# Moving 8 of 24 modulation tiles from the attention loop to the projection loop, and reordering three groups of loads

## What is computed

```python
def adaln(c, w, b):
    m = jax.nn.silu(c) @ w + b
    m = m.reshape(c.shape[0], 1, 6, D_MODEL)
    return [m[:, :, k] for k in range(6)]
...
    xp = xp + mp[2] * op
```

```python
def mla_sample(h, past_lat, past_rope, w_in, q_g, kv_g, w_qb, w_kvb, w_o):
...
    k_lat = jnp.concatenate([past_lat, ckv], axis=1)
    k_pe = jnp.concatenate([past_rope, kr], axis=1)
    q = jnp.concatenate([q_lat, q_pe], axis=-1)
    k = jnp.concatenate([k_lat, k_pe], axis=-1)[:, :, None, :]
    o_lat = causal_attention(q, k, k_lat[:, :, None, :], t0)
```

## Time and profile before

| | us |
|---|---|
| median of 3 runs | 1580.44 (1579.52 to 1583.05) |
| the profiled execution | 1581.58 |
| its span | 1580.0 |
| PE busy | 1494.8 |
| DVE, ACT, POOL busy | 370.3, 260.1, 111.2 |
| DMA | 463.22 MB, mean 293 GB/s |

### The profile page before, as it was taken

The page is one execution under the profiler, slowest core; times in us unless marked ns, Lnnn a source line. Parts: engine busy times, 40 slices in busy tenths (PEclk is TensorE's granted clock), DMA queues, the critical chain, the costliest instruction groups (busy, mean ns, idle before and its releaser), DMA issues.

```text
span 1580.0 us, 24287 instructions
## 1 busy us (share of the span) xinstructions
PE 1494.8 (95%) x9928; PEld 885.9 (56%) x9928; DVE 370.3 (23%) x903; ACT 260.1 (16%) x586; POOL 111.2 (7%) x167
## 2 busy tenths in 40 slices
PE   6999877999999999999998999999999999998998
PEld 3544545788888878778785554553344234432342
DVE  2223431300000055634576100001000100011104
ACT  2122320200000022357503100000000000000001
POOL 1101550000000000000010100000000100010000
PEclk9999997999999999999999999999999999999999
DMA  9759987244334553472358899999999999999995
GB/s 379 306 214 392 365 289 240 107 162 160 122 105 146 197 189 120 155 263 94 147 211 349 288 348 379 392 408 401 421 417 419 405 420 417 420 404 419 418 418 220
DMA packets 104011, 463.22 MB, mean 293 GB/s; under 512 B 16110, under 2 KB 35339, under 8 KB 62261
## 3 DMA queue, kind: packets, MB, share of 16 engines
q1 hardware_dynamic: 91136, 420.49, 68.7%
q0 software_dynamic: 10256, 39.98, 7.3%
q10 hardware_dynamic: 2512, 1.23, 0.3%
HBM read 446.30 MB, written 15.55 MB: 292 GB/s over the span
## 4 chain that ended last, share of the span: by engine, by line
PE 76%; DMA 11%; DVE 5%; issue 4%; POOL 2%; ACT 1%; SPq 0%; POOLq 0%; DVEq 0%
PE bank L1622 11%; PE bank L1177 10%; PE bank L1147 8%; PE bank L1672 5%; PE bank L1191 5%; PE bank L1515 5%; DMA ring<-in_moe_w_up 4%; DMA ringx<-in_moe_w_up 3%; PE bank L1634 3%; PE bank L1225 3%; PE bank L1530 2%; PE bank L1556 2%; PE bank L890 2%; PE bank L924 2%; PE bank L977 2%
## 5 line engine op out<-in xcount | busy, mean ns | idle before, releaser
L1622 PE MATMUL bank<-ring,hg 128*32 128x512 f32 (+1 forms) x1456 | 208.5, 566 | 7.8 <-DMA ring<-in_moe_w_up 7.1
L1177 PE MATMUL bank<-hT,ring 128*128 128x264 f32 x704 | 156.9, 386 | 0.3 <-ACT hT L1725 0.3
L1622 PE MATMUL bank<-ringx,hg 128*32 128x512 f32 (+1 forms) x848 | 146.1, 568 | 3.8 <-DMA ring<-in_moe_w_up 2.8
L1177 PEld LDWEIGHTS bank<-hT,ring 128*128 128x128 f32 x704 | 133.7, 190 | 23.4 <-issue 0.6
L1622 PEld LDWEIGHTS bank<-ring,hg 128*32 128x32 f32 x1456 | 62.7, 111 | 110.3 <-issue 99.8
L1147 PE MATMUL bank<-hT,ring 128*128 128x264 f32 x512 | 118.7, 394 | 1.7 <-ACT hT L1725 1.3
L1147 PEld LDWEIGHTS bank<-hT,ring 128*128 128x128 f32 x512 | 99.1, 194 | 19.9 <-issue 2.1
L1672 PE MATMUL bank<-ring,turnH 128*32 128x512 f32 x768 | 92.6, 603 | 0.0
L1191 PE MATMUL bank<-actT,ring 128*128 128x264 f32 x352 | 79.1, 386 | 0.6 <-DVE actT L2210 0.6
L1515 PE MATMUL bank<-ring,hg 128*128 128x512 f32 (+1 forms) x192 | 78.0, 560 | 0.6 <-ACT hg L1940 0.6
L1622 PEld LDWEIGHTS bank<-ringx,hg 128*32 128x32 f32 x848 | 44.2, 112 | 59.6 <-issue 55.8
(11 more groups left out here) (565 smaller groups left out, 1787.4 us busy)
## 6 DMA issues: line engine op xcount, KB each, us to landing
ring<-in_moe_w_down SPq DMA_DIRECT2D x53, 1024.0 KB, 17.1
ring<-in_w_ada SPq DMA_DIRECT2D x48, 1024.0 KB, 11.2
ring<-in_moe_w_up SPq DMA_DIRECT2D x40, 1024.0 KB, 16.1
ring<-in_moe_w_gate SPq DMA_DIRECT2D x32, 1024.0 KB, 17.0
ringx<-in_moe_w_gate SPq DMA_DIRECT2D x27, 1024.0 KB, 12.8
ringx<-in_moe_w_down SPq DMA_DIRECT2D x24, 1024.0 KB, 18.1
ring<-in_ssm_w_in SPq DMA_DIRECT2D x20, 1024.0 KB, 4.9
ringx<-in_moe_w_up SPq DMA_DIRECT2D x19, 1024.0 KB, 15.9
```

The source lines that it names most:

```text
L1177: m = mm(bank[2 * w + q][:, 0:T], slot8(tl)[:, k, q * P:(q + 1) * P], hT[:, k, :], start=k == 0, stop=k == DC - 1)
L1622: m = mm(bank[2 * b_ + u][rows, 0:HALVES[g][u]], hg[:, k, rows], w[:, kk, 512 * u:512 * u + HALVES[g][u]], start=k == 0, stop=k == DC - 1, ...
```

## The change

The diff does four things. It gives the projection loop 32 tiles (2 or 3 at a time) and four turns, with heads 3, 7, 11 and 15, and the attention loop 8 tiles (heads 0 to 7) and one turn (head 9). On POOL the rotary keys of group two are loaded ahead of the token pages of sequences 1 to 3. The token pages of sequence 7 go from SP's queue to POOL's, behind `samp_scored` 3. On SP the four tiles WO go behind the token pages of sequences 4 to 6, and so behind `samp_scored` 3 too.

```diff
--- before.py
+++ after.py
@@ -60,7 +60,7 @@
 
 MOE = 134
 LAT_SLOTS = [n % NS for n in range(LAT, WO)]
-ADA_HEADS = [(0, 2), (2, 4), (4, 6), (6, 7), (7, 8), (8, 8), (8, 10), (10, 12), (12, 14), (14, 15), (15, 16), (16, 16), (16, 18), (18, 20), (20, 22), (22, 24)]
+ADA_HEADS = [(0, 3), (3, 6), (6, 8), (8, 8), (8, 11), (11, 14), (14, 16), (16, 16), (16, 19), (19, 22), (22, 24), (24, 24), (24, 27), (27, 30), (30, 32), (32, 32)]
 MS = 12
 GROUPS = [(512 * g, min(512, FF - 512 * g)) for g in range(-(-FF // 512))]
 NG = len(GROUPS)
@@ -490,20 +490,20 @@
         flat = rvar[:, 0:256] if n >= 6 else spare[n // 2][:, 2048:2304]
         return flat[:, n % 2 * PAGE:(n % 2 + 1) * PAGE]
 
-    def page_ids(eng, b0):
-
-        return [[eng.value_load(pages[0:1, b * NPG + n:b * NPG + n + 1], min_val=0, max_val=a["cache_kv_latent"].shape[1] - 1)
-                 for n in range(NPG)] for b in range(b0, b0 + 4)]
+    def page_ids(eng, which):
+
+        return {b: [eng.value_load(pages[0:1, b * NPG + n:b * NPG + n + 1], min_val=0, max_val=a["cache_kv_latent"].shape[1] - 1)
+                    for n in range(NPG)] for b in which}
 
     def load_turned(eng, ids_, b, n):
 
         out = turned_page(b, n)
-        src = a["cache_kv_turned"][ds(ids_[b % 4][n], 1), :, :].rearrange("a p (u t) -> (a p) u t", u=4 if b == 3 else KC)
+        src = a["cache_kv_turned"][ds(ids_[b][n], 1), :, :].rearrange("a p (u t) -> (a p) u t", u=4 if b == 3 else KC)
         return eng.dma_start(out, src)
 
     def load_tokens(eng, ids_, b, n):
 
-        src = a["cache_kv_latent"][0, ds(ids_[b % 4][n], 1), :, :]
+        src = a["cache_kv_latent"][0, ds(ids_[b][n], 1), :, :]
         src = src.rearrange("a p (u r) -> (a p) u r", u=4) if b == 7 else src.rearrange("a p r -> (a p) r")
         return eng.dma_start(token_page(b, n), src)
 
@@ -560,19 +560,19 @@
             fill8(IN0 + j, w, win0[:, j, 0:DC * w])
         ada(0, ADAR, 1, 3)
         sp.wait_ge(s["pool_in"], 16)
-        sample_pages = page_ids(sp, 4)
+        sample_pages = page_ids(sp, range(4, NB))
         ada(1, ADA1, 0, 3)
         for b in range(4, NB):
             for n in range(NPG):
                 if n == 0:
                     sp.wait_ge(s["units"], unit(LAT + b - 4 - NS))
                 load_turned(sp, sample_pages, b, n).then_inc(ring_ready[(LAT + b - 4) % NS], 16)
+        sp.wait_ge(s["samp_scored"], 3)
+        for b in range(4, NB - 1):
+            for n in range(NPG):
+                load_tokens(sp, sample_pages, b, n).then_inc(lat_ready[b], 16)
         for j in range(4):
             fill8(WO + j, 256, wo_d[:, j, :])
-        sp.wait_ge(s["samp_scored"], 3)
-        for b in range(4, NB):
-            for n in range(NPG):
-                load_tokens(sp, sample_pages, b, n).then_inc(lat_ready[b], 16)
         with sp.Fori(0, 2) as i:
             for j in range(4):
                 for w, src in enumerate((wg0, wu0)):
@@ -705,7 +705,7 @@
         g.memset(qpeT[:, :, H:32], 0.0).then_inc(s["zeroed"], 1)
         g.memset(qlatT[:, :, :, H:32], 0.0).then_inc(s["zeroed"], 1)
 
-        sample_pages = page_ids(g, 0)
+        sample_pages = page_ids(g, (0, 1, 2, 3, 7))
 
         def turned(b):
             for n in range(NPG):
@@ -730,14 +730,16 @@
         rope_keys(0)
         g.wait_ge(s["s_done"], DC)
         tokens(0)
+        g.wait_ge(s["ada_turned"], 6)
+        g.wait_ge(s["rope_in"], 64 + 16 * NPG)
+        rope_keys(1)
         g.wait_ge(s["s_done"], H)
         tokens(1)
         tokens(2)
         g.wait_ge(s["o_done"], H)
         tokens(3)
-        g.wait_ge(s["ada_turned"], 6)
-        g.wait_ge(s["rope_in"], 64 + 16 * NPG)
-        rope_keys(1)
+        g.wait_ge(s["samp_scored"], 3)
+        tokens(7)
         g.wait_ge(s["ltok_copied"], 3)
         g.dma_start(o[2][0, 0].rearrange("(c p) r -> p c r", p=P), ltok[:, 0:2, 0:KVR]).then_inc(s["out_done"], 16)
         g.dma_start(o[3][0, 0].rearrange("(c p) r -> p c r", p=P), ltok[:, 0:2, KVR:]).then_inc(s["out_done"], 16)
@@ -995,8 +997,8 @@
                 if tile and tile % DC == 0:
                     pe.wait_ge(s["ada_added"], 1 + tile // DC)
                 ada_tile(ADAR + tile, tile % DC, bank[3])
-            if h in (5, 11):
-                ada_turn((5, 11).index(h) + 1, bank[3][:, 0:144])
+            if h % 4 == 3:
+                ada_turn(h // 4 + 1, bank[3][:, 0:144])
         head_back(H - 1)
 
 
@@ -1036,30 +1038,24 @@
                            start=t == 0, stop=t == 1, skip_group_check=True)
             m.then_inc(s["o_done"], 2)
 
-        pe.wait_ge(s["ada_added"], 3)
+        pe.wait_ge(s["ada_added"], 5)
         scores(0)
-
-        def ada1_turn(blk):
-            ada_turn(3 + blk, bank[2][:, 144 * blk:144 * (blk + 1)])
 
         for h in range(H):
             if h + 1 < H:
                 scores(h + 1)
-            t = DC + h
-            if t == 2 * DC:
-                pe.wait_ge(s["ada_copied"], 6)
-            ada_tile(ADA1 + t, t % DC, bank[(3, 7, 3)[t // DC]])
-            if t % DC == 1:
-                ada1_turn(t // DC - 1)
+            if h < DC:
+                ada_tile(ADA1 + 2 * DC + h, h, bank[3])
+            if h == DC + 1:
+                ada_turn(5, bank[2][:, 0:144])
             turn_p(h)
             if h % 2 == 0 and h:
                 values(h // 2 - 1)
-        ada1_turn(2)
         values(H // 2 - 1)
 
 
         pe.wait_ge(s["o_copied"], H // 2)
-        pe.wait_ge(s["ada_added"], 4)
+        pe.wait_ge(s["ada_added"], 6)
 
         def sample_scores(g_):
 
@@ -2106,13 +2102,12 @@
         v.wait_ge(s["rope_in"], 64)
         v.tensor_scalar(rope_rows[:], pages_all[:], float(ROPE), cst[:, C_ROW:C_ROW + 1], ALU.mult, ALU.add)
         for h in range(H):
-            if h in (4, 10, 15):
-                blk = (4, 10, 15).index(h) + 1
+            blk = h // 4 + 1
+            if h % 4 == 2:
                 ada_rows(blk, ADAR + DC * blk - 1, bank[3])
-            if h in (5, 11):
-                blk = (5, 11).index(h) + 1
+            if h % 4 == 3:
                 v.wait_ge(s["ada_turned"], blk + 1)
-                ada_add(0, bank[3][:, 0:144], 16 * blk, 16 * blk + 16, blk + 1)
+                ada_add(blk // 3, bank[3][:, 0:144], 16 * (blk % 3), 16 * (blk % 3) + 16, blk + 1)
             v.wait_ge(s["q_rotated"], h + 1)
             v.wait_ge(s["q_copied"], h + 1)
             v.tensor_tensor(ropet[64:96, :], bank[4][64:96, 0:T], sin, ALU.mult)
@@ -2145,9 +2140,8 @@
             if h + 1 < H:
                 maxima(h + 1)
             normalise(h)
-            t = DC + h
-            if t % DC == DC - 1:
-                ada_rows(3 + t // DC, ADA1 + t, bank[(3, 7, 3)[t // DC]])
+            if h == DC - 1:
+                ada_rows(5, ADA1 + 3 * DC - 1, bank[3])
             if h >= 3 and h % 2:
                 pair = h // 2 - 1
                 v.wait_ge(s["o_done"], 2 * pair + 2)
@@ -2155,7 +2149,7 @@
         v.wait_ge(s["o_done"], H)
         v.tensor_copy(oT[:, H // 2 - 1, 0:TP], bank[(H // 2 - 1) % 2][:, 0:TP]).then_inc(s["o_copied"], 1)
         v.wait_ge(s["ada_turned"], 6)
-        ada_add(1, bank[2][:, 0:432], 0, 48, 4)
+        ada_add(1, bank[2][:, 0:144], 32, 48, 6)
 
 
         def sample_sums(g_):
```

## The result

The change makes the kernel slower: 1590.95 us in the median of 10 runs (1587.49 to 1595.73), against 1583.59 (1578.03 to 1589.18) for the kernel before, run beside it. The ratio is 1.0048, with a 95% interval of 1.0032 to 1.0065. The forecast was 1573.5, in a range of 1569 to 1581. The profiled execution took 1590.72 us with a span of 1588.8, 8.8 more than the span before.

What follows compares the result with a forecast made beforehand. It took PE's path to bound the kernel (76% of the chain), with a 12.2 us wait for rotary keys. +9.2 − 2.1 − 14.0 = −6.9 us, from the median 1580.44, gave 1573.5 us, range 1569 to 1581.

Steps and rivals of the forecast that it cites:

- the part on the attention loop: Attention loop: heads 8 to 14 gain nothing from losing a tile; last head and last turn save, sum −2.1 us.
- The first rival: Second half of attention loop: clock falls, 1.5 us a head, +12 for 8, so 1585.5 us; chance 10%.
- Projection loop, +9.2: Projection loop: 10 more tiles and one more turn cost +10.3 us, less 1.1 at its end.
- Last head and last turn, −2.1: End of attention loop: tile delaying transposes 1.0, turn holding values 0.85, shorter addition 0.3 us, all saved.
- Rotary wait, −12.2: Before second scoring of the sequences: PE's 12.2 us wait for rotary keys of group two goes whole.
- the clock of the second scoring, −1.8: `sample_scores(1)`: clock stays up without the wait, so 9.0 us instead of 10.8.
- Moved loads, 0, bound +5.1: Group two's token pages, WO, sequence 7: moving them costs nothing; pages at most 5.1 us late.
- the second rival: Values of group two: token pages come late, PE stands still, +1.5 to +5.1, 1575 to 1578.6 us; chance 18%.
- Supply of tiles, 0, bound +3: Projection loop: tiles behind SP's page numbers arrive in time with 2 us to spare; cost 0, at most +3.
- the sum −6.9: Whole kernel: +9.2 projection loop, −2.1 attention loop, −14.0 rotary keys and second scoring's clock.

Runs made afterwards that it cites:

- the second group: Four follow-up kernels run on one chip beside the kernel before: four idle products 0.9992, sequence 7 on SP 0.9982, output weights ahead 0.997, five idle products 0.9977.
- the third group: Four kernels run again unchanged on one chip beside the kernel before: seven idle products 0.9964, four 0.9969, own memory for rotary keys 0.991, that with five products 0.9926.

## Why the prediction was wrong

**The step that failed** is in the part on the attention loop: heads 8 to 14 "lose a tile each and gain nothing: the gap is only idle for 1.6 us". The gap was idle for 1.6 us, and PE's order of work stood as forecast. But the clock was taken to stay at 1.00. The first rival came instead. Its size was well priced in the sum: 12, against 10.7 + 2.1 = 12.8 measured for the loop. A pair took 11.05 − 7.4 = 3.65 us more, so 1.8 a head and not 1.5; but the clock fell late in the first of the eight heads, and the last has no scores of its own. The rival had left out 2.1 more for the first scoring: the low clock outlasted the gaps by some 5 us, with PE busy all the time (240 to 244). What was wrong was its chance of 10%. It rested on one row, 66 to 68 us in the earlier trace rows, with PE busy for 0.66 of 2 us at full clock: one gap by itself. Eight heads without a tile are another case. No row of the kernel before could have settled it. One of its stretches has PE almost as little busy as the change at 196 to 200 (2.72 of 4 us), and keeps its clock:

```profile
204.00:208.00 4.00, 2.85 (x24) 1.66 (x21) 2.34 (x10) 2.16 (x9) 0.00 (x0) 1.00 0.60 164
```

And with the tiles alone PE was busy 9.92 of 16 us at 1.00 before the clock fell. That the missing tiles are the cause is shown by the kernels with products in their place: 26.28 of 32 us busy at 1.00, with the same work of DVE and the same loads.

The Trainium skill, TensorE: Matmul & The Clock Gate, section A second HAM failure mode: psum-queue depth-cycling, says that frequent short idle times between groups of matmuls can make the clock go up and down. The trace agrees with the cause and not quite with the picture: 44 us at 0.50 in one piece (about 201 to 245), with no rise in between.

**Projection loop, +9.2:** right, with a little luck. The first scores came at 165.59, which is 7.8 later, and 1.35 of the start is to be added: +9.2. A third tile of a head took 0.86 us (2.71 for three, 1.85 for two), not 0.925, and a wait of 0.55 for a tile, counted as nothing, made up for most of that.

**Last head and last turn, −2.1:** right as far as it can be read. With products in the gaps the loop takes 62.0 us against 63.7 − 2.1 = 61.6.

**Rotary wait, −12.2, and the clock of the second scoring, −1.8:** right, both to a tenth.

**Moved loads, 0, bound +5.1:** low by 1.3 (1.9 for the whole stretch); this is the second rival, at its low end. The sum had 4.2 MB at 342 GB/s, 12.3 us from the end of the first scoring. But SP took 13.1 us to issue 24 of the pages, the last landed 5.4 later, and PE went on 18.2 us after the start, at 269.42. The engines moved 289 to 305 GB/s at a share of 1.01 to 1.07; why less than 342 stays open. It was counted at no transfer time saved by a second issuer, with reference to the Trainium skill, DMA: Bandwidth & Descriptors, section Issuing engines are not separate DMA queues. The rule leaves the issue time to be saved, and that was worth 2.2 us of waiting when it was taken away, as SP alone left the engines at 0.78.

**Supply of tiles, 0, bound +3:** 2 us were to spare by the sum, and yet PE waited 0.55 us for one tile. That is within the bound.

**The size of the gain itself:** the sum −6.9 plus the failed step (12.8 + 2.1) plus late pages (1.9) less the earlier start (1.35) is +8.6. The forecast in us has one more error: it stood on 1580.44, the median of three runs of the kernel before, and ten gave 1583.59. Of the 17.4 us between 1573.5 and 1590.95, 3.1 are this base.

And the larger lesson of the runs: the tiles need not have moved. The keys of group two hung on the turn of block 5 only through the memory they share. Another place for them gives the 12.2 us without the 9.2 of the projection loop.

## What to carry to other kernels

A small piece of work in an idle gap of TensorE may be holding its clock. Before moving it, price the low clock over all that follows, not over the gap, and give that outcome more than a small chance: a stretch of the old trace that kept its clock with as little work did not rule it out here. After moving it, look at the granted clock; four idle products were enough here to win back 12 us. When a load waits for a buffer, look first for other memory, and only then for a new order of the work. Take an idle product's price from a row: where it is longer than the gap, it costs more than it saves.

## What was not expected of the hardware

**When the clock falls is not fixed.** PE's same instructions had it fall in the first bare gap (200.9 us) in the change and in the fourth (216.9) with the loads of before. With every second gap filled it did not fall in the loop in one execution and did, behind a stall, in another. And two kernels that ran twice, unchanged, differ at one place each: the first scoring of the one with seven products (3.52 or 1.85 us for the same 16 products), the output projection of the one with five (7.39 or 9.07 us for the same 32).

**VectorE stood still for 5 to 8 us.** In the second group all four kernels have a stretch like this in DVE's timeline, 7.6 to 7.9 us in three of them and 5.4 in the fourth:

```profile
204.62 0.42 DVE L2137 TENSOR_REDUCE mx<-bank 128x1 f32<-128x256 f32 x1 [7.91 <-remote]
```

PE, with its scores ready, stood still for 4.7 us of it, and the clock fell for some 7 us behind it (0.55 and 0.60 from 204 to 212). Two of the four kernels ran again in the third group, on another chip, and had none of it: the one with products ahead of the output projection went from 0.9977 to 0.9926, the one with four products in the loop from 0.9992 to 0.9969. So it does not belong to the instructions of the kernel alone; chip and time of the run changed together, and which of them counts is not shown. Nor do all kernels lose alike: from the third group to the second these two lose 14 and 8 us, the kernel before, of which no trace was kept there, 4.6. The ratios of the second group are therefore too high, and above only its traces and its times among each other are used. What DVE waited for is open: the trace names no releaser on the core. The DMA engines were at 0.87 and 0.74 of their time in the 8 us around it. They carry instruction loads too (79 and 29 packets in two queues of their own in the profile of the change); whether one of these came late was not tried.
